# Attention over heads in pairs: two heads on two partition halves, inverse sums applied to the outputs

## The reference

```python
def rms_norm_2(x, g):                       # over the 64 columns of a head
    return x * lax.rsqrt(jnp.mean(x * x, -1, keepdims=True) + EPS) * g
...
def neighbourhood_attention(q, k, v, k_ctx, v_ctx, rpb):
    ...
        s_w = einsum('bjhd,brjchd->bhjrc', q_i, k_w) * scale + bias     # window and a bias table
        s_c = einsum('bjhd,bnhd->bhjn', q_i, k_ctx) * scale             # 256 context keys
        p = softmax(concatenate([s_w, s_c], -1))
        o = p @ [v_w; v_ctx]
...
def window_attention(...):                  # 2 key heads, 4 query heads on each, a window of +-128
    ...
        p = sink_softmax(concatenate([s_w, s_c], -1), sink)   # exp(sink - m) joins the sum
...
def context_attention(q, k, v, sink):       # layer 0 only: the 256 context queries see context keys
```

## Time and profile before

| | |
|---|---|
| median of 3 runs | 4388.82 us (4381.26 to 4393.31) |
| the profiled execution | 4390.56 us, of which span 4389.3 us |
| TensorE busy | 4033.6 us (92%) |
| VectorE, ScalarE, GpSimd busy | 2358.2, 1531.6, 1212.2 us |
| mean granted TensorE clock | 0.948 |

### The profile page before, as it was taken

One profiled execution on the slowest core, in us unless ns is written; L12 is line 12 of the kernel. 1 busy time (PEld: TensorE's weight loads), 2 busy tenths in 40 slices (PEclk: granted clock), 3 DMA queues, 4 the chain that ended last, 5 costly groups with the idle time before them and its releaser, 6 DMA issues.

```text
span 4389.3 us, 54130 instructions
## 1 busy us (share of the span) xinstructions
PE 4033.6 (92%) x21044; PEld 3275.9 (75%) x21044; DVE 2358.2 (54%) x4000; ACT 1531.6 (35%) x2626; POOL 1212.2 (28%) x793
## 2 busy tenths in 40 slices
PE   5999778889998999888998899989999989999999
PEld 4888557788888888568887675778868866668777
DVE  6555773566557786546335788421364358630452
ACT  3223333443234223444233223433254232343352
POOL 1113333242024113024013229123202332514214
PEclk8999889999999999999999897999999989999999
DMA  7565224235554564214324110011101111112102
GB/s 263 171 199 148 87 88 143 93 125 185 185 175 151 171 198 135 70 53 143 93 90 125 39 48 31 24 40 61 53 15 32 65 48 58 40 34 92 63 17 94
DMA packets 131598, 433.13 MB, mean 99 GB/s; under 512 B 14480, under 2 KB 14480, under 8 KB 130704
## 3 DMA queue, kind: packets, MB, share of 16 engines
q1 hardware_dynamic: 130912, 427.04, 30.0%
q10 hardware_dynamic: 432, 2.62, 0.1%
HBM read 427.51 MB, written 2.10 MB: 98 GB/s over the span
## 4 chain that ended last, share of the span: by engine, by line
PE 76%; DVE 14%; issue 4%; ACT 3%; POOL 2%; DMA 1%; SPq 0%; DVEq 0%; ACTq 0%; POOLq 0%
PE ps L594 19%; PE ps L595 19%; PE ps L596 19%; PE ps L1631 5%; PE ps L1650 4%; DVE cut L1933 3%; PE ps L1640 2%; PE ps L620 1%; PE ps L622 1%; PE ps L621 1%; DVE cut L1143 1%; PE ps L1866 1%; DVE cut L995 1%; POOL cut L523 1%; ACT cut L513 1%
## 5 line engine op out<-in xcount | busy, mean ns | idle before, releaser
L594 PE MATMUL ps<-cut 128*128 128x512 f32 (+1 forms) x5216 | 1877.5, 360 | 175.9 <-POOL cut L523 40.8
L595 PE MATMUL ps<-cut 128*128 128x512 f32 (+1 forms) x5216 | 1837.6, 352 | 0.0
L596 PE MATMUL ps<-cut 128*128 128x512 f32 (+1 forms) x5216 | 1834.9, 352 | 0.0
L594 PEld LDWEIGHTS ps<-cut 128*128 128x128 f32 x5216 | 1014.3, 194 | 338.8 <-issue 114.2
L523 POOL TENSOR_TENSOR cut<-cut 128x1024 fp32r<-128x1024 f32 (+3 forms) x334 | 734.1, 2201 | 1500.9 <-ACT cut L513 1500.3
L595 PEld LDWEIGHTS ps<-cut 128*128 128x128 f32 x5216 | 1015.5, 195 | 131.8 <-issue 6.6
L596 PEld LDWEIGHTS ps<-cut 128*128 128x128 f32 x5216 | 1014.1, 194 | 126.2
L513 ACT ACTIVATE cut<-cut 128x1024 fp32r<-128x1024 f32 (+3 forms) x680 | 630.9, 936 | 592.8 <-PE ps L596 476.0
L523 DVE TENSOR_TENSOR cut<-cut 128x1024 fp32r<-128x1024 f32 (+2 forms) x346 | 420.0, 1216 | 445.7 <-ACT cut L513 445.7
L841 POOL TENSOR_TENSOR cut<-cut 128x512 fp32r<-128x512 f32 (+1 forms) x100 | 136.9, 1369 | 1012.6 <-ACT cut L801 1012.6
L1933 DVE SCALAR_TENSOR_TENSOR cut<-cut,cols 128x512 f32<-128x512 f32 (+1 forms) x330 | 281.1, 852 | 11.7
(11 more groups left out here) (259 smaller groups left out, 3763.0 us busy)
## 6 DMA issues: line engine op xcount, KB each, us to landing
cut<-in_ffn_in SPq DMA_DIRECT2D x200, 512.0 KB, 3.8
cut<-in_mod_w SPq DMA_DIRECT2D x128, 512.0 KB, 4.2
cut<-in_ffn_out SPq DMA_DIRECT2D x96, 384.0 KB, 3.3
cut<-in_ffn_out SPq DMA_DIRECT2D x96, 320.0 KB, 3.0
cut<-in_w_ada SPq DMA_DIRECT2D x48, 512.0 KB, 3.5
cut<-in_w_merge SPq DMA_DIRECT2D x48, 512.0 KB, 3.4
cut<-in_even_in SPq DMA_DIRECT2D x36, 512.0 KB, 3.5
cut<-in_proj SPq DMA_DIRECT2D x48, 256.0 KB, 2.6
```

The source lines that it names most:

```text
L594: te.matmul(o, hi[:, k - ka, w], xs[0], start=k == 0, stop=False)
L595: te.matmul(o, hi[:, k - ka, w], xs[1], start=False, stop=False)
L596: ins = te.matmul(o, lo[:, k - ka, w], xs[0], start=False, stop=last)
```

## The change

A job is now two heads and one block of queries (24 jobs and 16). Scores, exponentials and maxima of the two heads lie side by side in one buffer of 2 x 768. On TensorE the two heads' scores follow each other on partition halves, and so do their value products, on the two halves of the output columns. The exponentials are no longer multiplied by the inverse sum: TensorE multiplies the inverse sum, broadcast as 64 columns, by the identity (line 1732 of the changed kernel), which leaves it in 128 further columns of the output's bank, and VectorE multiplies the output by that (1807) after ScalarE has copied the output to SBUF (1763). The context columns of both heads are transposed into one bank and copied by VectorE (1803), the window columns by ScalarE (1760). Two groups of taps follow each job. The head sums go to four groups of 32 rows, from four square buffers. A bias table load is made for each head as before, one pair of buffers in layer 0, two in layer 1. The first block's attention keeps its instructions.

```diff
+    def stat(i, k, s=None):
+        o = 8 * (i % 4) + 2 * k
+        return st[:, o:o + 2] if s is None else st[:, o + s:o + s + 1]
+    def pe_pairs(tag, jobs):
+        n = len(jobs)
+        for i in range(n + 3):
+            if i < n:
+                J, w = jobs[i], jobs[i]["w"]
+                for s in range(2 if w else 0):
+                    b = bank["p_s", tag, i, s] = yield from pe_take(("v_max", tag, i, s))
+                    te.matmul(PS[b][:, 0:w], J["q"][s], J["k"][s], start=True, stop=True).then_inc(*sig("p_s", tag, i, s))
+                for s in range(2):
+                    b = bank["p_sx", tag, i, s] = yield from pe_take(("v_max", tag, i, 2 + s))
+                    te.matmul(PS[b][:, 0:256], J["q"][s], J["kx"][s], start=True, stop=True).then_inc(*sig("p_sx", tag, i, s))
+            if 0 <= i - 2 < n:
+                w, sbuf = jobs[i - 2]["w"], SBUFS[(i - 2) % 3]
+                for s in range(2 if w else 0):
+                    te.wait_ge(*(yield "a_exp", tag, i - 2, s))
+                    b = bank["p_t", tag, i - 2, s] = yield from pe_take(("a_pt", tag, i - 2, s))
+                    for k in range(0, w, 128):
+                        ins = te.transpose(PS[b][:, k:k + 128], sbuf[:, s, k:k + 128], ident)
+                    ins.then_inc(*sig("p_t", tag, i - 2, s))
+                b = bank["p_tx", tag, i - 2] = yield from pe_take(("v_pt", tag, i - 2))
+                for s in range(2):
+                    te.wait_ge(*(yield "a_exp", tag, i - 2, s))
+                    for k in range(0, 256, 128):
+                        ins = te.transpose(PS[b][:, 256 * s + k:256 * s + k + 128], sbuf[:, s, w + k:w + k + 128], ident)
+                ins.then_inc(*sig("p_tx", tag, i - 2))
+            if 0 <= i - 3 < n:
+                J, w, pbuf = jobs[i - 3], jobs[i - 3]["w"], PBUFS[(i - 3) % 2]
+                b = bank["p_pv", tag, i - 3] = yield from pe_take(("v_o", tag, i - 3))
+                te.wait_ge(*(yield "v_rsum", tag, i - 3))
+                for s in range(2):
+                    te.matmul(PS[b][64 * s:64 * s + 64, 128:256], stat(i - 3, 2, s).to_broadcast([128, 64]), ident, start=True, stop=True)
+                for s in range(2 if w else 0):
+                    te.wait_ge(*(yield "a_pt", tag, i - 3, s))
+                te.wait_ge(*(yield "v_pt", tag, i - 3))
+                nv = len(J["v"][0])
+                for k in range(nv):
+                    for s in range(2):
+                        ins = te.matmul(PS[b][64 * s:64 * s + 64, 0:128], J["v"][s][k], pbuf[:, s, k * 128:(k + 1) * 128],
+                                        start=k == 0, stop=k == nv - 1)
+                ins.then_inc(*sig("p_pv", tag, i - 3))
...
+    def act_pairs(tag, jobs):
+        n = len(jobs)
+        for i in range(n + 3):
+            if i < n:
+                J, sbuf = jobs[i], SBUFS[i % 3]
+                se.wait_ge(*(yield "v_nmax", tag, i))
+                for s in range(2):
+                    x = sbuf[:, s, 0:J["w"] + 256]
+                    se.activation(x, x, ACT.Exp, bias=stat(i, 1, s), accum_out=stat(i, 2, s)).then_inc(*sig("a_exp", tag, i, s))
+                for s in range(2 if J["sink"] else 0):
+                    se.activation(stat(i, 3, s), J["sink"][s], ACT.Exp, bias=stat(i, 1, s)).then_inc(*sig("a_sink", tag, i, s))
+            if 0 <= i - 2 < n:
+                w, pbuf = jobs[i - 2]["w"], PBUFS[(i - 2) % 2]
+                for s in range(2 if w else 0):
+                    se.wait_ge(*(yield "p_t", tag, i - 2, s))
+                    if i >= 4:
+                        se.wait_ge(*(yield "p_pv", tag, i - 4))
+                    se.activation(pbuf[:, s, 0:w], PS[bank["p_t", tag, i - 2, s]][:, 0:w], ACT.Copy).then_inc(*sig("a_pt", tag, i - 2, s))
+            if 0 <= i - 3 < n:
+                se.wait_ge(*(yield "p_pv", tag, i - 3))
+                se.activation(jobs[i - 3]["out"], PS[bank["p_pv", tag, i - 3]][:, 0:128], ACT.Copy).then_inc(*sig("a_av", tag, i - 3))
...
+    def dve_pairs(tag, jobs, between=lambda i: nothing(i)):
+        n = len(jobs)
+        for i in range(n + 3):
+            if i < n:
+                J, w, sbuf = jobs[i], jobs[i]["w"], SBUFS[i % 3]
+                if i >= 3:
+                    ve.wait_ge(*(yield "p_tx", tag, i - 3))
+                for s in range(2 if w else 0):
+                    ve.wait_ge(*(yield "p_s", tag, i, s))
+                    if J["table"]:
+                        ve.wait_ge(*(yield J["table"][s]))
+                    ve.tensor_tensor_reduce(sbuf[:, s, 0:w], PS[bank["p_s", tag, i, s]][:, 0:w], J["mask"][s], 1.0, J["first"][s],
+                                            ALU.add, ALU.max, stat(i, 0, s)).then_inc(*sig("v_max", tag, i, s))
+                for s in range(2):
+                    ve.wait_ge(*(yield "p_sx", tag, i, s))
+                    if w:
+                        ve.wait_ge(*(yield "v_max", tag, i, s))
+                    ve.tensor_tensor_reduce(sbuf[:, s, w:w + 256], PS[bank["p_sx", tag, i, s]][:, 0:256], con("causal", 0, 256),
+                                            1.0, stat(i, 0, s) if w else J["first"][s], ALU.add, ALU.max,
+                                            stat(i, 0, s)).then_inc(*sig("v_max", tag, i, 2 + s))
+                ve.wait_ge(*prev("v"))
+                if i >= 4:
+                    ve.wait_ge(*((yield "a_sink", tag, i - 4, 1) if jobs[i - 4]["sink"] else (yield "a_exp", tag, i - 4, 1)))
+                ve.tensor_scalar(stat(i, 1), stat(i, 0), -1.0, None, ALU.mult).then_inc(*sig("v_nmax", tag, i))
+            if 0 <= i - 1 < n:
+                sm = stat(i - 1, 2)
+                if jobs[i - 1]["sink"]:
+                    ve.wait_ge(*(yield "a_sink", tag, i - 1, 1))
+                    ve.tensor_tensor(sm, sm, stat(i - 1, 3), ALU.add).then_inc(*sig("v_sum", tag, i - 1))
                     ve.wait_ge(*prev("v"))
                 else:
+                    ve.wait_ge(*(yield "a_exp", tag, i - 1, 1))
                 ve.reciprocal(sm, sm).then_inc(*sig("v_rsum", tag, i - 1))
+            if 0 <= i - 2 < n:
+                w, pbuf = jobs[i - 2]["w"], PBUFS[(i - 2) % 2]
+                ve.wait_ge(*(yield "p_tx", tag, i - 2))
+                if i >= 4:
+                    ve.wait_ge(*(yield "p_pv", tag, i - 4))
+                ve.tensor_copy(pbuf[:, :, w:w + 256], PS[bank["p_tx", tag, i - 2]][:, :].rearrange("p (a n) -> p a n", a=2)).then_inc(*sig("v_pt", tag, i - 2))
+            if 0 <= i - 3 < n:
+                o = jobs[i - 3]["out"]
+                ve.wait_ge(*(yield "a_av", tag, i - 3))
+                ve.tensor_tensor(o, o, PS[bank["p_pv", tag, i - 3]][:, 128:256], ALU.mult).then_inc(*sig("v_o", tag, i - 3))
             yield from between(i)
...
-                te.matmul(PS[b][0:8, 0:n], sel[t], t512[o + t % 2][:, 0:n], start=t == 0, stop=t == 3).then_inc(*sig("p_hs", key, gi, t))
+                te.matmul(PS[b][32 * t:32 * t + 32, 0:n], sel, t512[o + t][:, 0:n], start=True, stop=True).then_inc(*sig("p_hs", key, gi, t))
...
-                if t >= 2:
-                    se.wait_ge(*(yield "p_hs", key, gi, t - 2))
-                elif gi:
-                    se.wait_ge(*(yield "p_hs", key, gi - 1, 3))
-                se.activation(t512[o + t % 2][:, 0:n], x[:, t, g[0]:g[1]], ACT.Square).then_inc(*sig("a_hsq", key, gi, t))
+                if gi:
+                    se.wait_ge(*(yield "p_hs", key, gi - 1, t))
+                se.activation(t512[o + t][:, 0:n], x[:, t, g[0]:g[1]], ACT.Square).then_inc(*sig("a_hsq", key, gi, t))
             se.wait_ge(*(yield "p_hs", key, gi, 3))
-            se.activation(t512[o + 2 + gi][0:8, 0:n], PS[bank["p_hs", key, gi]][0:8, 0:n], ACT.Sqrt, bias=epsc(EPS)[0:8],
+            se.activation(t512[o + 4 + gi][:, 0:n], PS[bank["p_hs", key, gi]][:, 0:n], ACT.Sqrt, bias=epsc(EPS),
...
-                te.matmul(PS[b][:, 0:n], back[t], t512[o + 2 + gi][0:8, 0:n], start=True, stop=True).then_inc(*sig("p_hb", key, t, gi))
+                te.matmul(PS[b][:, 0:n], back[t], t512[o + 4 + gi][32 * t:32 * t + 32, 0:n], start=True, stop=True).then_inc(*sig("p_hb", key, t, gi))
...
-        yield from dve_attention(("na", l), na_jobs(l), lambda i: dve_taps(l, 1))
+        yield from dve_pairs(("na", l), na_jobs(l), lambda i: dve_taps(l, 2))
...
-        for h in range(8):
-            if h >= 2:
-                sy.wait_ge(*(yield "v_max", ("na", l), (6 if l == 0 else 4) * (h - 2) + 3, 0))
-            sy.dma_start(tt_sb[:, 896 * (h % 2):896 * (h % 2 + 1)], a["rpb"][l, h]).then_inc(*dsig(f"d_tt{h % 2}", l, h))
+        for t in range(4):
+            last, per = t - (2 if l else 1), 4 if l else 6
+            for s in range(2):
+                if last >= 0:
+                    sy.wait_ge(*(yield "v_max", ("na", l), per * last + 3, s))
+                sy.dma_start(table_at(l, t)[:, 896 * s:896 * (s + 1)], a["rpb"][l, 2 * t + s]).then_inc(*dsig(f"d_tt{s}{t % 2}", l, t))
```

(16 more changed lines are left out.)

181 lines of the change are left out of this document (77 added, 104 removed).

## The result

The changed kernel takes 4262.7 us (median of 4 runs, 4259.07 to 4267.43) against 4391.07 us (4 runs beside it): ratio 0.9712, 95% interval 0.9693 to 0.9731. The forecast was 4337 us with a range from 4300 to 4378, so the sign was right and the size was not: 128 us less instead of 52. The profiled execution took 4263.1 us, 127.5 less than the one of before.

A forecast was written before the change was run, and what follows sets the result against it. TensorE was taken to bound the kernel, and after the change a chain through VectorE and ScalarE in attention. Attention saves 37 us, head sums and scales 15: 4390.6 - 37 - 15 = 4338.6, as median 4337, range 4300 to 4378.

The forecast's parts named there:

- The ring: Attention job as closed chain: maxima, negate, exponentials, copies, output copy, multiply; 6.03 us a pair with 512 window columns.
- the clock's surcharge: Attention stages: TensorE partly falling to 1.2 GHz and becoming the bound again there, +30 us.
- The clock takes some back: Attention stages: a less busy TensorE partly runs at 1.2 GHz, +30 us, so attention saves 37 instead of 66.9.
- Full clock throughout: Rival, 20%: TensorE keeps its full clock in attention; 4302 us.
- What is late next: Attention: each job's length is its chain over VectorE and ScalarE, 6.03 us a pair; stages 466.3 us at full clock.
- Head sums and scales: Outside attention: four square buffers save 5 to 12 us, spreading on four row groups 0 to 15; 15 taken together.
- 0 to 15: Saving in us allowed for the head sums' spreading (1866), whose products on four row groups can overlap.
- TensorE's part shrinks: Attention: paired heads overlap on TensorE, so a pair takes 4.6 us, or 6.1 without value overlap, against 7.48.
- values do not overlap: Rival, 10%, beside the others: value passes not overlapped, TensorE 6.1 us a pair, costing 5 to 10 us.
- Slower: Rival, 7%: the 1.2 GHz level holds through the attention stages, 561 us for them; 4407 us in all.
- the ring costs more than its parts: Rival, 15%: hand-overs of 0.2 instead of 0.05 us, or disturbed PSUM reads, some 0.8 us on 80 jobs; about 4370.
- the signs named in advance: Trace marks: VectorE idle before 1807, ScalarE before 1751, exponentials 6.0 us apart, stages about 170, 121, 108, 96 us.

The follow-up runs named there:

- experiment 7: Changed kernel with the convolution's taps on VectorE placed ahead of the multiply of a job's output instead of behind it: 4255.5 us, 0.9698.
- experiment 5: Changed kernel with the head sums' squares through two buffers instead of four, the new strips kept: 4274.4 us, 0.9744.
- Experiments 1 and 6: Changed kernel with the output multiply moved: 1, one job later, behind that job's maxima and negate, 4223.5 us; 6, between the two kinds of maxima, 4221.0 us.
- Experiment 4: Changed kernel with the head sums and their spreading put back as in the kernel before, pairs of heads kept: 4295.9 us, 0.9790.
- experiment 2: Changed kernel with all value products of the first head issued before those of the second, not alternating: 4283.3 us, 0.9762.

## Why the prediction was wrong

The ring was right as a mechanism and wrong in its length; the clock's surcharge was wrong as a mechanism; the head sums were priced too low. All three missed in the same direction: 96.0 + 31.5 us measured against 37 + 15. No one term would have saved the forecast: without the clock's 30 us it stands at 4309, still 46 us above the profiled execution. The range missed because no case in it had a ring shorter than the sum of its parts, or more than 20 us from head sums and scales.

**"The clock takes some back" (+30 us) is the step that failed in kind.** The clock did fall, as forecast, in parts of every stage. But jobs did not get longer by it. Windows of one whole period each (negation to negation) in window attention, two of the same kind in layer 1 and then two in layer 0:

```profile
4051.98:4056.96 4.98, 4.93 (x55) 4.08 (x57) 3.00 (x14) 2.97 (x10) 0.00 (x0) 1.00 0.00 0
4072.43:4077.40 4.97, 4.97 (x46) 3.96 (x45) 2.99 (x13) 2.80 (x9) 0.00 (x0) 0.75 0.02 5
3232.89:3237.06 4.17, 4.17 (x38) 3.04 (x36) 2.10 (x10) 2.80 (x9) 0.00 (x0) 0.72 0.01 2
3259.31:3263.48 4.17, 3.35 (x40) 2.44 (x38) 2.10 (x10) 2.80 (x9) 0.00 (x0) 1.00 0.00 0
```

The last two have the same 4.17 us at a granted clock of 0.72 and of 1.00: at the lower one TensorE was busy throughout, at the higher one for 3.35 us. I had priced the 1.2 GHz level as if whole tiles ran at it, so that TensorE's 8.4 us a pair set the time. It held for parts of single jobs there, and what it used up was TensorE's slack. (The first window, near the start of its stage, has more of TensorE's work in it, 55 records against 46, so the second pair is the cleaner one.) Whole stages show the same where an experiment left their instructions as they were: window attention of layer 0 in experiment 7, then neighbourhood attention of layer 1 in experiment 5:

```profile
3161.60:3265.50 103.90, 91.20 (x786) 67.27 (x787) 65.61 (x279) 58.33 (x201) 0.00 (x0) 0.87 0.00 1
3686.60:3787.30 100.70, 84.16 (x770) 61.82 (x771) 57.82 (x202) 49.75 (x113) 41.20 (x50) 0.90 0.11 38
```

At a mean clock of 0.87 and 0.90 they took 103.9 and 100.7 us, in the changed kernel 103.6 and 101.4 at 0.92 and 0.95. The measured periods, put into the forecast's own count of jobs with its taps of 41.3 and 7.7 us, give 437.8 us for the four stages; measured are 437.2. That leaves next to nothing for the clock in the sum, that of the tap jobs included. It was the 20% rival "Full clock throughout" that had this right in effect, though not in its condition, since the clock was 0.84 to 0.95 over the stages. The Trainium skill, TensorE: Matmul & The Clock Gate, "A second HAM failure mode: psum-queue depth-cycling", right behind the section that the prediction quoted, tells of a bf16 kernel whose clock swings because of frequent short gaps between groups of matmuls, and whose throughput suffers by it. The trace agrees with the fall (0.75 and 0.72 over jobs of window attention, where TensorE waited for ScalarE 2.0 us at most at a time, not the 1.4 us of the forecast), and shows no cost in these jobs.

**"What is late next" was right in kind, and 0.36 us a pair too long (29 us).** Each link stands in the timeline above. Maxima 2.15 us against 2.42: they start 0.61 and 0.41 apart, although they last 0.69 and 0.48, because the next one starts before the last has ended; I had taken the lengths. The trace of before held the shorter steps: each maximum's read-out starts 0.61 and 0.41 us behind it (the maxima themselves, at 2773.84 and 2774.68, stand in the earlier trace rows):

```profile
2774.45 0.08 DVE L1695 DVE_READ_ACCUMULATOR2_ANT st<- 128x1 f32 x1
2775.09 0.08 DVE L1695 DVE_READ_ACCUMULATOR2_ANT st<- 128x1 f32 x1
```

Output copy to multiply to next maximum is 0.31 + 0.20 = 0.51 (the latter from 3741.94 to 3742.14) against 0.60, for the same reason. Exponentials 1.85 against 1.88, copies 0.95 against 0.94, negation to exponential 0.21 against 0.19. Sum 5.67 against 6.03. Window attention was off by 0.38 to 0.39 (5.25 against 5.63, 4.98 against 5.37 in layer 1). Over the stages at full clock the forecast was 466.3, the measurement 437.2: 29 us. Experiments 1 and 6 show that the ring is the cause and not a likeness: the same instructions in another order took 39 and 42 us less.

**"Head sums and scales" (15 us) was half of what it is.** Experiment 4 puts it at 28 to 33, experiment 5 splits it. The buffers were priced rightly at 5 to 12. The bounds "0 to 15" for the spreading were too low: I looked only at products that overlap in one stretch, while six stretches lost 26 us together. Even both upper bounds, 12 + 15, fall short of the 31.5 measured.

**"TensorE's part shrinks"** held. Scores and value passes overlap in pairs; experiment 2 shows what that is worth for the values, 0.92 us a job on TensorE and 21 us of the kernel, and that a job of the steady ring had room for it. The rival "values do not overlap" would have cost more than its 5 to 10 us even so.

**"Slower" and "the ring costs more than its parts"** did not come: both hand-overs between VectorE and ScalarE measured 0.04 us (the negation starts at 3744.29 and lasts 0.17, the exponential starts at 3744.50; the output copy starts at 3747.30 and lasts 0.27, the multiply starts at 3747.61).

Of the signs named in advance, VectorE idle ahead of 1807 (2.49 us) and ScalarE ahead of 1751 (2.59 us) came as described; the stages came at 153, 103, 101 and 80 us and not near 170, 121, 108 and 96. The exponentials of successive jobs start 5.67 us apart and not 6.0.

The sum again with measured sizes: ring terms 29 us, clock 30 us, head sums some 16 us: 75 us, which is the whole distance between 4338.6 and 4263.1.

## What to carry to other kernels

When a change relieves the busiest engine, write the next bound as a closed chain through the in-order queues, from start to start and not from lengths, and then look for an order of the same instructions that opens it: here one instruction moved by half a job was worth 42 us, a third of what the whole change brought (128). Buffers close chains as well as waits do, so look in each new order for a second ring through the bank that it holds longer. A lower clock on an engine with slack was no cost here (4.17 us a job at a mean of 0.72 and at 1.00), so price it only where that engine would set the period for longer than its slack lasts.

## What was not expected of the hardware

- Successive max reductions on VectorE start 0.61 us apart at 512 columns and 0.41 at 256, while their own rows last 0.69 and 0.48.
- Value passes on the two column halves run beside each other in fp32: 24 passes in 1.41 us if they alternate, where twelve of one head took 1.45 before, and 2.33 if each half's come in a row.
- In window attention TensorE spent parts of jobs at the 1.2 GHz level (means of 0.72 and 0.75 over a job) although it had waited for ScalarE no longer than 2.0 us at a time, and was at 1.00 in other jobs of the same kind; the period was the same at either.
